# Fillers of the stick-breaking, retention and sliding-window stages in quarters instead of halves

## What is computed

```python
h = _rms(x, norm1_g) * valid
z = h @ w_in                      # all inputs of the mixers, and four gates of 1024 channels
y_sb  = stick_breaking_attention(...)
y_ret = silu(bg) * retention(...)
y_rw  = rwkv7_mix(...)
y_sw  = sliding_window_attention(...)
merged = sum(sigmoid(gate_i) * (y_i @ p_i) for the four branches)
x = x + merged @ w_o
x = x + squared_relu_mlp(_rms(x, norm2_g))
```

## Time and profile before

| | |
|---|---|
| median of 3 runs | 1204.14 us (1203.28 to 1204.44) |
| the profiled execution | 1203.32 us, span 1201.6 us |
| PE / DVE / ACT / POOL busy | 98% / 42% / 41% / 39% |
| granted TensorE clock | full (1.00) |
| chain that ended last | PE 82%, DVE 10%, ACT 5%, POOL 2%, issue 2% |

### The profile page before, as it was taken

How to read it: one execution, slowest core, us unless ns; L and a number is a source line. 1 busy time by engine, 2 the same in 40 slices (tenths; PEclk the granted TensorE clock), 3 DMA queues, 4 the chain that set the end, 5 groups by cost and what they waited for, 6 DMA issues and landing times.

```text
span 1201.6 us, 20666 instructions
## 1 busy us (share of the span) xinstructions
PE 1175.7 (98%) x8782; PEld 962.4 (80%) x8782; DVE 502.9 (42%) x994; ACT 489.8 (41%) x808; POOL 468.5 (39%) x288
## 2 busy tenths in 40 slices
PE   8999999999999899999999999999999999999998
PEld 7998877887788578667777787778888888888887
DVE  4799435454554553533362585272522000222000
ACT  6455323222323443776635634443643312243210
POOL 3443435325443125323342532353334544344541
PEclk9999999999999999999999999999999999999999
DMA  6222323222222142211522221242232323232330
GB/s 250 89 73 86 116 80 107 65 76 96 89 73 72 35 146 65 65 36 71 197 88 62 86 76 53 73 174 88 70 105 88 123 92 102 70 106 88 123 123 35
DMA packets 35998, 111.47 MB, mean 93 GB/s; under 512 B 4273, under 2 KB 9137, under 8 KB 35394
## 3 DMA queue, kind: packets, MB, share of 16 engines
q1 hardware_dynamic: 30288, 98.59, 24.5%
q10 hardware_dynamic: 5106, 11.43, 2.7%
q0 software_dynamic: 512, 0.13, 0.1%
HBM read 99.43 MB, written 9.04 MB: 90 GB/s over the span
## 4 chain that ended last, share of the span: by engine, by line
PE 82%; DVE 10%; ACT 5%; POOL 2%; issue 2%; DMA 0%; DVEq 0%; ACTq 0%
PE pst L1843 18%; PE pst L1845 17%; PE pst L1844 17%; PE pst L2019 5%; PE pst L2017 5%; PE pst L2018 5%; POOL w_lo L814 1%; PE pst L2358 1%; ACT w_hi L932 1%; PE pst L2350 1%; PE pst L2136 1%; PE pst L2083 1%; PE pst L2320 1%; PE pst L2335 1%; DVE cdif L1411 1%
## 5 line engine op out<-in xcount | busy, mean ns | idle before, releaser
L814 POOL TENSOR_TENSOR w_lo<-raw,w_hi 128x1024 fp32r<-128x1024 f32 x164 | 402.3, 2458 | 634.0 <-ACT w_hi L932 622.3
L1843 PE MATMUL pst<-h_hi,w_hi 128*128 128x512 f32 (+1 forms) x704 | 255.5, 363 | 1.3 <-DVE h_lo L1384 0.7
L1845 PE MATMUL pst<-h_hi,w_lo 128*128 128x512 f32 (+1 forms) x704 | 242.8, 345 | 0.0
L1844 PE MATMUL pst<-h_lo,w_hi 128*128 128x512 f32 (+1 forms) x704 | 242.5, 344 | 0.0
L932 ACT ACTIVATE w_hi<-raw 128x1024 fp32r<-128x1024 f32 x164 | 171.9, 1052 | 140.2 <-PE pst L2019 114.2
L1843 PEld LDWEIGHTS pst<-h_hi,w_hi 128*128 128x128 f32 x704 | 133.1, 189 | 25.4 <-issue 5.7
L1845 PEld LDWEIGHTS pst<-h_hi,w_lo 128*128 128x128 f32 x704 | 132.9, 189 | 15.9
L1844 PEld LDWEIGHTS pst<-h_lo,w_hi 128*128 128x128 f32 x704 | 133.2, 189 | 15.1 <-issue 2.2
L1843 PE MATMUL pst<-x_hi,w_hi 128*128 128x512 f32 (+1 forms) x272 | 102.6, 377 | 0.4 <-DVE x_lo L1715 0.4
L1844 PE MATMUL pst<-x_lo,w_hi 128*128 128x512 f32 (+1 forms) x272 | 102.4, 377 | 0.0
L1845 PE MATMUL pst<-x_hi,w_lo 128*128 128x512 f32 (+1 forms) x272 | 102.4, 376 | 0.0
(11 more groups left out here) (339 smaller groups left out, 2022.7 us busy)
## 6 DMA issues: line engine op xcount, KB each, us to landing
raw<-in_weights SPq DMA_DIRECT2D x164, 512.0 KB, 3.3
xt<-in_x SPq DMA_DIRECT2D x4, 512.0 KB, 5.0
wait_gate<-stage ACTq DMA_DIRECT2D x8, 256.0 KB, 2.7
gate_t<-wait_gate ACTq DMA_DIRECT2D x1, 2048.0 KB, 9.4
x<-in_x ACTq DMA_DIRECT2D x1, 2048.0 KB, 7.9
out<-x SPq DMA_DIRECT2D x7, 256.0 KB, 3.6
cst<-in_consts SPq DMA_DIRECT2D x1, 1524.0 KB, 10.7
wait_ret_g<-stage ACTq DMA_DIRECT2D x4, 256.0 KB, 3.0
```

The lines of the kernel that those rows point to most:

```text
L814: nc.gpsimd.tensor_tensor(w_lo[:, u % W_SLOTS, :], raw[:, u % RAW_SLOTS, :], w_hi[:, u % W_SLOTS, :].bitcast(F32), ALU.subtract).then_inc( ...
L1843: M(out, lh, rh, start=(first and i == 0), stop=False)
L1844: M(out, lh, rl, start=False, stop=False)
L1845: last = M(out, ll, rh, start=False, stop=(final and i == len(terms) - 1))
```

## The change

A gate is cut into 4 pieces and a projection into 2, so a piece of these jobs has 6 matmuls. All counts of fillers from the stick-breaking stage to the sliding window are doubled, except that heads 1, 3 and 5 of stick-breaking have five pieces in front of their sums instead of four, and that `ret_prep`'s `pieces`, the last count of `RET_POST_FILL` and `SW_END_FILL` are 3 instead of 4. The number of matmuls in all is the same. TensorE's part of a projection is written for two parts: `job_begin` and the wait for the branch's output at part 0, and `dense_done` at part 1.

```diff
-SB_FILL = [(2, 0)] * 7 + [(2, 2)]
+SB_FILL = [(4, 0), (5, 0)] * 3 + [(4, 0), (4, 4)]
 SB_E = 3
-RET_FILL = [(2, 1)] * 5
-RET_POST_FILL = [(0, 1), (1, 2), (1, 2), (2, 2)]
-SW_FILL = [(2, 2)] + [(1, 2)] * 6 + [(1, 1)]
-SW_END_FILL = 2
+RET_FILL = [(4, 2)] * 5
+RET_POST_FILL = [(0, 2), (2, 4), (2, 4), (4, 3)]
+SW_FILL = [(4, 4)] + [(2, 4)] * 6 + [(2, 2)]
+SW_END_FILL = 3
...
-PARTS = {**dict.fromkeys(("aq", "ak", "bq", "bk", "bg", "dq", "dk", "rgate"), 4), "bv": 2, "bdv": 3, "gate": 2}
+PARTS = {**dict.fromkeys(("aq", "ak", "bq", "bk", "bg", "dq", "dk", "rgate"), 4), "bv": 2, "bdv": 3, "gate": 4, "proj": 2}
...
             g("ret_prep")
-            pieces(2)
+            pieces(3)
             g("ret_gate")
...
                 elif kind == "proj":
-                    s = job_begin(n)
-                    pe.wait_ge(yl_ready, y_count(a) + 4)
+                    s = job_slot(n)
+                    if part == 0:
+                        job_begin(n)
+                        pe.wait_ge(yl_ready, y_count(a) + 4)
                     us = u % W_SLOTS
                     ws = [slice(2 * P * k + P * (b % 2), 2 * P * k + P * (b % 2) + P) for k in range(4)]
-                    product3(pst[:, 2 * s, :], [((w_hi[:, us, ws[k]], w_lo[:, us, ws[k]]), (y_hi[:, k, :], y_lo[:, k, :]))
-                                                for k in range(4)]).then_inc(dense_done, 1)
+                    last = product3(pst[:, 2 * s, :],
+                                    [((w_hi[:, us, ws[k]], w_lo[:, us, ws[k]]), (y_hi[:, k, :], y_lo[:, k, :]))
+                                     for k in range(2 * part, 2 * part + 2)], part == 0, part == 1)
+                    if part == 1:
+                        last.then_inc(dense_done, 1)
```

## The result

The changed kernel takes 1230.68 us (median of 4 runs, 1230.08 to 1232.34) against 1203.84 before (4 runs on the same chip, 1203.28 to 1204.44): a ratio of 1.0225, 95% interval 1.0207 to 1.0243. It is slower by 26.8 us, where 19.6 had been forecast, and lies just above the upper end of the range. The profiled execution took 1231.02 us with a span of 1229.3, 27.7 above that of before.

What follows compares the result with a forecast made beforehand. TensorE, busy 98% at full clock, was taken to bound the kernel. Heads +12.1, before retention 0, first retention block +3.9, last norm -1.4, window +7.2 and -0.8, behind it -1.4 gave +19.6: 1223.7 us, range 1217 to 1230.

Steps and rivals of the forecast that it cites:

- slot wait in head 1, 2, 3: Stick-breaking heads: TensorE waits for VectorE to drain the projection two jobs before, in the same PSUM slot; 3.6, 2.7, 5.0 us.
- no wait in head 5: Stick-breaking head 5 has only gates, drained by ScalarE, so no slot wait; +0.3 us for the head.
- wait for the reload: Before retention, TensorE reaches the key transposes early and waits 1.4 us for the same landing; net 0.
- wait for the decayed keys: Retention's second block: the later gate delays the keys' norm and decay, so TensorE waits; +3.9 us, bounds +2.5 and +5.5.
- sliding window, three waits: Last quarter of three window blocks asks for a projection finished in the same block; 2.4 us each, together +7.2.
- time added in the heads, at full clock: Stick-breaking stage: +11.85 us through head 3 and +0.3 in head 5, sum +12.1, bounds 11 and 13.
- window, other waits: Sliding window: today's one TensorE wait in a transposition, 0.8 us, was taken as gone because its gate ends earlier.
- The sum goes by the full clock: Whole kernel: the added waits were priced with TensorE at the full 2.4 GHz, nothing added for a slower clock.
- rival A: Clock falls to 1.2 GHz behind one or two of the three longest waits; about 1226.5 us; chance 0.20.
- B: Only the slot waits in the heads hold, ScalarE and VectorE having slack later; +9.3, 1213.4 us; chance 0.10.
- C: Faster: head 1's drain is in time, so no slot or norm wait comes; about 1201 us; chance 0.03.
- D: Whole kernel: no difference, by waits and gains that cancel; chance 0.02.

Runs made afterwards that it cites:

- the kernel with all waits filled: The changed kernel with idle matmuls in front of all seven new waits (heads 1 to 3, retention, sliding window); median 1222.41 us, ratio 1.0162.
- the early drain: The changed kernel with VectorE draining the first finished projection of heads 1 to 3 inside the sums' chain; 1216.53 us, ratio 1.0106.
- the quarters alone: The kernel before with the finer cut and every count exactly twice the old one, no head with five; 1204.35 us, ratio 1.0001.

## Why the prediction was wrong, point by point

| step | forecast, us | measured, us |
|---|---|---|
| slot wait in head 1, 2, 3 | 3.6, 2.7, 5.0 | 3.48, 2.56, 4.92 |
| no wait in head 5 | yes | yes |
| wait for the reload | 1.4 | 1.60 |
| wait for the decayed keys | 3.9 | 4.12 |
| sliding window, three waits | 2.4 each | 2.53; 1.39 and 0.25; 1.79 |
| time added in the heads, at full clock | +12.1 | +12.1 |
| before retention | 0 | -0.2 (+0.3 in the changed kernel) |
| first retention block | +3.9 | +4.3 |
| behind the last norm | -1.4 | -1.4 |
| window, the three places | +7.2 | +7.3 |
| window, other waits | -0.8 | -1.6 |
| behind the window | -1.4 | -1.4 |
| all of it at full clock | +19.6 | +19.1 in the profiles, +19.7 in runs side by side |
| the clock | 0 | 8.0 |

The lower rows compare the profile of the kernel with all waits filled, whose clock was full, with that of before, place by place.

**The waits** were right in place, releaser and nearly in length. The reason given, a drain that stands behind the sums in VectorE's queue and hangs on the scores, is shown by the early drain; that of the retention wait by moving the gate; that of the window by moving a quarter. In the window the forecast's 2.4 is a distance from start to start, so it compares with the costs 2.8, 2.2 and 2.2 and not with the brackets; the sum is right because the first came out too short and the others too long. In the heads two small errors cancel too: heads 1 to 3 come out 0.3 longer than forecast, and head 5 gains 0.5 at the mask instead of 0.2, so its +0.3 doesn't come. Not foreseen was a gain of 0.6 by the window's first transposition.

**The step that failed** is "The sum goes by the full clock." The text weighed that nothing in the trace of before was as long as head 3's 5.0, and gave rival A, the fall, 0.20. It fell behind all four of the long waits, 8.0 us together, head 2's 2.56 among them, which rival A did not name. That is the size of rival A's far end ("with the same at the others up to 8"), which was left out of the range. The argument "only one much so" measured these waits against one of 2.9 us at full clock. But that wait stands at the very start, before the first matmul; between matmuls, the longest wait of the kernel before is this one:

```profile
438.52 0.39 PE L1843 MATMUL pst<-w_hi,h_hi 128*128 128x256 f32 x1 [1.62 <-DVE sb_vm L1477]
```

So the trace of before held nothing like the new waits, and four of them, not one, were much longer. The profiles also show that for waits of 2.5 us the clock differs from one execution to the next, so a single one shows little. The rule named beside it (the Trainium skill, "TensorE: Matmul & The Clock Gate", HAM oscillation: an idle gap can halve the clock, and the work behind it starts cold) agrees with this case's trace: 0.50 in 484 to 488, behind 3.48 us of idleness. In head 2 and in retention the trace differs from it in one point: the work behind the gap began at full clock and fell about a microsecond later. By that rule, priced from rival A's rows, the sum would have been near 1226 to 1232, and it should have carried the forecast.

**Rivals.** B (only the head waits hold) is out, since retention and window waited as written; C and D are out too. "TensorE's busy time stays, apart from the clock" held: 8.7 more, about the clock's 8.0.

## What to carry to other kernels

When a change of order moves the point at which a place in the program asks for a buffer, find the release of that buffer in its engine's queue and what that hangs on; three of such waits were right here to 0.15 us, and cost about 0.3 more than the idle time that the profile shows. Then price each wait twice, once for its own length and once for a halved clock behind it, and let the range hold the second: here it was 40% on top, and behind one and the same retention wait of 4.1 us it was 1.6 to 2.9 us in four profiles. Here a fifth piece paid where the job before it in the slot had ended in an earlier head, as with the gates of heads 5 and 7.

## What was not expected of the hardware

- The granted clock fell to 0.50 at every idle wait of 3.5 to 4.9 us in the profiles, eleven in six kernels, but at waits of 1.25 to 2.6 us in some profiles and not in others. What decides is open.
- This is part of the scatter of the kernel before. At the same place and after the same wait, 1.28 us ahead of the window's second scores, its profile and that of the quarters alone differ (the first row is of before, the second of the other kernel):

```profile
676.00:680.00 4.00, 4.00 (x30) 3.36 (x27) 2.28 (x4) 2.07 (x9) 3.71 (x6) 1.00 0.32 101
```

```profile
676.00:680.00 4.00, 4.00 (x25) 3.25 (x23) 2.33 (x4) 2.08 (x9) 3.71 (x6) 0.64 0.30 103
```

- Matmuls whose result nobody uses made a kernel faster, by 4 us in three places and 8 in seven (medians of different experiments), by holding the clock through waits that they didn't shorten.
